# Row operands of TensorE as high and low part on two partitions, in one fp32r matmul

## What is computed

```python
# FoX: cum = cumsum(log_sigmoid(forget logits)), one row of 256 for each of 16 heads
s = einsum('bhqd,bhkd->bhqk', q_b, k) * scale
s = s + c_b[..., :, None] - cum[..., None, :]
# router: bias added to the logits of every token
p_group = softmax(xf @ wr_g + br_g);  e_logits = xf @ wr_e + br_e
# mixer: input projection with bias, q, k, v, o and others from column ranges of it
px = (rmsnorm(x, g) * (1 + sc1) + sh1) @ w_in + b_in
# mLSTM, chunk of 128: running maximum m_t of the log weights, decay to the state before
a = b + m;  Dlog = b[t] - b[s] + i[s];  m_t = max(a, max_s Dlog)
w_inter = exp(a - m_t);  s = (q k) * exp(Dlog - m_t)
num = w_inter * (q C) + s v;  den = w_inter * (q n) + sum(s)
```

## Time and profile before

| | us |
|---|---|
| median of three runs | 2669.48 |
| lowest, highest | 2665.62, 2684.37 |
| the profiled execution | 2661.06 |
| its span, first to last instruction | 2659.3 |

### The profile page before, as it was taken

One profiled execution on the slowest core, in us unless ns is written; L12 is line 12 of the kernel. 1 busy time (PEld: TensorE's weight loads), 2 busy tenths in 40 slices (PEclk: granted clock), 3 DMA queues, 4 the chain that ended last, 5 costly groups with the idle time before them and its releaser, 6 DMA issues. The chain is left out here.

```text
span 2659.3 us, 45347 instructions
## 1 busy us (share of the span) xinstructions
PE 2299.1 (86%) x19616; PEld 1828.5 (69%) x19616; DVE 1154.5 (43%) x2041; ACT 884.4 (33%) x1471; POOL 58.3 (2%) x78
## 2 busy tenths in 40 slices
PE   6999688888796799887999999886896998996998
PEld 6957465665462787675767676553766998866998
DVE  4344635323320552545323232333756554755554
ACT  4423232133210443332222221322534443534442
POOL 0000000000000000000000000000000000000000
PEclk9988898898998899988999999887888999988999
DMA  6575698899999556847999999976503644404650
GB/s 225 159 242 204 222 384 336 332 369 391 402 388 398 192 188 227 292 156 280 394 394 386 393 393 379 394 276 235 197 17 109 224 167 145 139 5 141 208 167 24
DMA packets 254368, 676.25 MB, mean 254 GB/s; under 512 B 12624, under 2 KB 65872, under 8 KB 254160
## 3 DMA queue, kind: packets, MB, share of 16 engines
q1 hardware_dynamic: 238832, 614.74, 62.5%
q0 software_dynamic: 15328, 58.50, 6.5%
HBM read 672.15 MB, written 1.05 MB: 253 GB/s over the span
## 5 line engine op out<-in xcount | busy, mean ns | idle before, releaser
L434 PE MATMUL bank<-xx,high 128*128 128x256 f32 (+1 forms) x3296 | 634.3, 294 | 59.5 <-DVE xx L570 37.1
L434 PEld LDWEIGHTS bank<-xx,high 128*128 128x128 f32 (+1 forms) x3296 | 524.6, 195 | 117.3 <-issue 76.7
L434 PE MATMUL bank<-xx,low 128*128 128x256 f32 (+1 forms) x1648 | 475.8, 289 | 0.0
L434 PEld LDWEIGHTS bank<-xx,low 128*128 128x128 f32 (+1 forms) x1648 | 321.8, 195 | 1.6
L385 DVE TENSOR_TENSOR low<-lane,high 128x1024 fp32r<-128x1024 f32 (+1 forms) x112 | 130.7, 1170 | 374.6 <-ACT high L376 374.6
L376 ACT ACTIVATE high<-lane 128x1024 fp32r<-128x1024 f32 (+1 forms) x112 | 112.9, 1012 | 334.0 <-PE bank L434 334.0
L434 PE MATMUL bank<-hx,high 128*128 128x256 f32 x1056 | 200.6, 291 | 6.3 <-DVE low L385 6.3
L434 PEld LDWEIGHTS bank<-hx,high 128*128 128x128 f32 x1056 | 166.5, 193 | 24.2 <-issue 15.2
L434 PE MATMUL bank<-hx,low 128*128 128x256 f32 x528 | 150.4, 285 | 0.0
L1229 ACT ACTIVATE hs<-bank 64x256 f32<-64x256 f32 x64 | 24.2, 377 | 312.3 <-PE bank L1216 312.2
L1236 DVE TENSOR_TENSOR hs<-hs,bank 64x256 f32<-64x256 f32 x64 | 27.1, 423 | 222.7 <-ACT hs L1229 222.5
(11 more groups left out here) (510 smaller groups left out, 4211.4 us busy)
## 6 DMA issues: line engine op xcount, KB each, us to landing
ring__11<-in_expert_w_gu SPq DMA_DIRECT2D x52, 1024.0 KB, 11.1
ring__10<-in_expert_w_gu SPq DMA_DIRECT2D x51, 1024.0 KB, 11.4
ring__12<-in_expert_w_gu SPq DMA_DIRECT2D x51, 1024.0 KB, 11.0
ring__50<-in_expert_w_gu SPq DMA_DIRECT2D x26, 1024.0 KB, 10.7
ring__10<-in_expert_w_down SPq DMA_DIRECT2D x26, 1024.0 KB, 9.1
ring__150<-in_expert_w_gu SPq DMA_DIRECT2D x26, 1024.0 KB, 12.0
ring__49<-in_expert_w_gu SPq DMA_DIRECT2D x25, 1024.0 KB, 10.8
ring__12<-in_expert_w_down SPq DMA_DIRECT2D x25, 1024.0 KB, 9.7
```

The source lines that it names most:

```text
L434: done = pe.matmul(out, a.bitcast(F32R), b.bitcast(F32R), start=it["start"] and k == 0 and q == 0 and not halves, stop=stop)
```

## The change

The row operands are put on two partitions (or two groups of them), as a high part rounded to fp32r and a low part, and one fp32r matmul adds both.

* **Inputs.** `row` arrives in a scratch tile, every bias on two partitions. ScalarE rounds all of it (128x1024), VectorE multiplies it by 0 or 1 on even or odd partitions (`odd`) and combines both (`flip` is +1 or -1): the even partition keeps the high part, the odd one gets the rest. FoX now waits for this last instruction (`stack`). ScalarE also makes fp32r copies of `ones` and of a new table `pick` (-1 where the partition modulo 32 is the head).
* **FoX.** `cum_s` holds the high part of cum and, 32 partitions on, the low part, for both halves; `pick` selects both and turns the sign. VectorE has a copy of 128x256 and two differences of 16x256 for one product of 128x256.
* **Mixer.** The directions sit at partitions 0 and 64 instead of 0 and 32. `nw` gets high parts at q0 and low parts at q0 + 32. A gate chain has four more instructions (18 counted steps for 14), with one more wait in each chunk. ScalarE clears `nw` (128x512) at the head of each mixer.
* `sgub` keeps an fp32 matmul, of two rows instead of one. `graw` becomes part of `tm`, and the context mixer shares the MoE's `rs`.

```diff
         def R(name, a=0, n=None):
             q, o, wd = ROW[name]
-            return row[q:q + 1, o + a:o + (wd if n is None else a + n)], ones[q:q + 1, :]
+            return row[q:q + 2, o + a:o + (wd if n is None else a + n)].bitcast(F32R), ones_r[q:q + 2, :].bitcast(F32R)
+        def picked(q, rows, h):
+            return pick[q:q + 32 + rows, h:h + 1].bitcast(F32R).to_broadcast([32 + rows, P])
...
             def act(act):
                 act.wait_ge(*vec_in.at("row"))
+                act.activation(ones_r.bitcast(F32R), ones, ACT.Copy)
+                act.activation(pick.bitcast(F32R), V("pick"), ACT.Copy)
                 act.activation(zeros.bitcast(F32R), V("mask_z"), ACT.Copy).then_inc(*zero_a.up("zeros"))
...
+                act.activation(rows_h.bitcast(F32R), rows, ACT.Copy).then_inc(*row_a.up("high"))
...
+                dve.tensor_scalar(rows_o, rows, V("odd"), None, MUL).then_inc(*row_v.up("odd"))
+                dve.wait_ge(*row_a.at("high"))
+                dve.wait_ge(*row_v.at("odd"))
+                dve.scalar_tensor_tensor(row.bitcast(F32R), rows_h, V("flip"), rows_o, MUL, ADD).then_inc(*row_v.up("stack"))
...
-            return room, [(x_out_a, ("in", 7)), (x_out, ("in", 6))], dict(sp=sp, pe=pe, act=act, dve=dve, pool=pool)
+            return room, [(x_out_a, ("in", 7)), (row_v, "stack")], dict(sp=sp, pe=pe, act=act, dve=dve, pool=pool)
...
-                    sel = ident[q0:q0 + H, q0 + h:q0 + h + 1]
-                    n = pe.matmul(sv[:, j, :], sel.to_broadcast([H, P]), ncum[q0:q0 + H, 0:nk], start=False, stop=True)
+                    n = pe.matmul(sv[:, j, :], picked(q0, H, h), cum_s[q0:q0 + 32 + H, 0:nk].bitcast(F32R), start=False, stop=True)
...
-                        dve.tensor_scalar(ncum, cum, -1.0, None, MUL).then_inc(*cum_v.up("ncum"))
+                        dve.tensor_copy(cum_s.bitcast(F32R), cum).then_inc(*cum_v.up("high"))
+                        dve.wait_ge(*cum_v.at("high"))
+                        for q0 in (0, 64):
+                            n = dve.tensor_tensor(cum_s[q0 + 32:q0 + 32 + H, :].bitcast(F32R), cum[q0:q0 + H, :], cum_s[q0:q0 + H, :], SUB)
+                        n.then_inc(*cum_v.up("ncum"))
...
-                pe.matmul(bank[:, 0:64], one, bc(rb[:, 4:36], [1, 2, 32], 1), start=True, stop=False, skip_group_check=True)
+                pe.matmul(bank[:, 0:64], one, bc(rb[:, 4:36], [2, 2, 32], 1), start=True, stop=False, skip_group_check=True)
...
             def decay_pe(pe, i, hp):
-                q0 = 32 * d
+                q0 = 64 * d
...
-                    sel = ident[q0:q0 + 4, q0 + h:q0 + h + 1].to_broadcast([4, P])
-                    n = pe.matmul(bank[:, 256 * j:256 * j + 256], sel, nw[q0:q0 + 4, a].rearrange("p c t -> p (c t)"), start=True, stop=True)
+                    n = pe.matmul(bank[:, 256 * j:256 * j + 256], picked(q0, 4, 2 * hp + j),
+                                  nw[q0:q0 + 36, a].rearrange("p c t -> p (c t)").bitcast(F32R), start=True, stop=True)
...
             def act(act):
                 events_wait(act, opened)
+                act.activation(nw.rearrange("p a c t -> p (a c) t").bitcast(F32R), bc(V("mask_z"), [P, 4, P], 1), ACT.Copy).then_inc(
+                    *gate_a.up(K("zero")))
                 norm.squares(act, 0)
...
-                    step(dve.tensor_scalar(NW[:, a, 0, :], MT[:, s0:s1], -1.0, None, MUL))
-                    yield
-                    step(dve.tensor_scalar(NW[:, a, 1, :], MT[:, s0:s1], -1.0, prev, MUL, ADD))
+                    step(dve.tensor_copy(NH[:, a, 0, :].bitcast(F32R), MT[:, s0:s1]))
+                    yield
+                    step(dve.tensor_scalar(NH[:, a, 1, :].bitcast(F32R), MT[:, s0:s1], prev, None, SUB))
+                    ready()
+                    step(dve.tensor_tensor(NL[:, a, 0, :].bitcast(F32R), MT[:, s0:s1], NH[:, a, 0, :], SUB))
+                    step(dve.scalar_tensor_tensor(NL[:, a, 1, :].bitcast(F32R), MT[:, s0:s1], prev, NH[:, a, 1, :], SUB, SUB))
```

More of the change, by code:

```diff
@@ L47 @@
                   ("mask_z", 128), ("mask_ge", 128), ("mask_le", 128), ("tri", 128), ("ones", 128), ("iota", 64), ("zero", 1),
-                  ("eps", 1), ("jota", NX)):
+                  ("eps", 1), ("jota", NX), ("flip", 1), ("odd", 1), ("pick", 16)):
     _vec(_name, _w)
@@ L160, in build @@
         vec = space(ctx, "vec", NVEC)
-        row = space(ctx, "row", NROW)
+        row, ones_r, pick = space(ctx, "row", NROW), space(ctx, "ones_r", P), space(ctx, "pick", 16)
         mods = space(ctx, "mods", 256)
@@ L192, in build @@
         zero_a = sig("zeros")
+        row_a, row_v = sig("rows_high"), sig("rows")
         tr_x, x_out = sig("x_turned"), sig("x_copied")
@@ L716, in inputs @@
             xin, cin = room("xin", 2, DM), room("cin", 2, DM)
+            rows, rows_h, rows_o = room("rows", NROW), room("rows_h", NROW), room("rows_o", NROW)
             groups = [(s, d, a, c) for s, d in ((xin, x), (cin, xr[:, :, 0:T])) for a in range(2) for c in (0, 4)]
@@ L720, in sp @@
                 sp.dma_start(vec, A["vec"]).then_inc(*vec_in.up("vec", 16))
-                sp.dma_start(row, A["row"]).then_inc(*vec_in.up("row", 16))
+                sp.dma_start(rows, A["row"]).then_inc(*vec_in.up("row", 16))
                 sp.dma_start(xin, A["x"][0].rearrange("(a p) d -> p a d", p=P)).then_inc(*x_in.up("x", 16))
@@ L776, in fox @@
             cum, ncum, wf = room("cum", T), room("ncum", T), room("wf", KC, P)
+            cum_s = room("cum_s", T)
             mod = Modulation(0, room)
@@ L1384, in pe @@
                 rb, one = R("br", 36 * L, 36)
-                pe.matmul(bank[:, 0:64], one, bc(rb[:, 4:36], [1, 2, 32], 1), start=True, stop=False, skip_group_check=True)
-                pe.matmul(bank[:, 64:72], one, bc(rb[:, 0:4], [1, 2, 4], 1), start=False, stop=False, skip_group_check=True)
+                pe.matmul(bank[:, 0:64], one, bc(rb[:, 4:36], [2, 2, 32], 1), start=True, stop=False, skip_group_check=True)
+                pe.matmul(bank[:, 64:72], one, bc(rb[:, 0:4], [2, 2, 4], 1), start=False, stop=False, skip_group_check=True)
                 pe.wait_ge(*rstd.at(norm.name))
@@ L1892, in norm_turns, with mixer @@
                     yield
-        def mixer(L, v, get, part, room, bk, opened, npairs, wide, rate, deep, early_in=None, x_ready=None, xx=None):
+        def mixer(L, v, get, part, room, bk, opened, npairs, wide, rate, deep, early_in=None, x_ready=None, xx=None, rs=None):
             K = lambda *k: (L, v, *k)
@@ L1977, in mixer @@
             end = len(proj.items) - 1
-            in_done = [(ev_a, proj.out(at_[where[-1]], last_o, 1)), (gate_v, K(0, 14)), (gate_v, K(1, 14)), (lastm_v, K(1))]
+            in_done = [(ev_a, proj.out(at_[where[-1]], last_o, 1)), (gate_v, K(0, 18)), (gate_v, K(1, 18)), (lastm_v, K(1))]
             if not states_only:
@@ L2038, in sgu_pe @@
                             pe.matmul(o, sv[:, a, g * 64:(g + 1) * 64], wst[:, g, :], start=True, stop=False, tile_position=(0, q0))
-                            n = pe.matmul(o, R("sgub")[1][:, 0:64], R("sgub", 512 * L + g * P, P)[0], start=False, stop=True,
+                            n = pe.matmul(o, ones[96:98, 0:64], R("sgub", 512 * L + g * P, P)[0].bitcast(F32), start=False, stop=True,
                                           tile_position=(96, q0))
@@ L2183, in gate_logs_act @@
                 for d in range(2):
[L2184 removed]
+                    B = rB[64 * d:64 * d + 4, :]
                     act.wait_ge(*gate_a.at(K(d, "exp")))
[L2186 removed]
+                    act.activation(B, B, ACT.Ln, bias=ones[64 * d:64 * d + 4, 0:1]).then_inc(*gate_a.up(K(d, "ln")))
             def conv_ln_act(act, which):
@@ L2334, in gate_chain @@
                 B, U, MT = (r_[q0:q0 + 4, :] for r_ in (rB, rU, rM))
-                NW, on4 = nw[q0:q0 + 4], ones[q0:q0 + 4, 0:1]
+                NH, NL, on4 = nw[q0:q0 + 4], nw[q0 + 32:q0 + 36], ones[q0:q0 + 4, 0:1]
                 dve.wait_ge(*gr_a.at(K(2 * d + 1)))
@@ L2772, in context_mixer @@
         def context_mixer(room, lane, bk, rs):
-            s = mixer(0, 0, room, room.part, lane, bk, [], 2, 256, 7, 1)[2]
+            s = mixer(0, 0, room, room.part, lane, bk, [], 2, 256, 7, 1, rs=rs)[2]
             def pool(e):
@@ L2950, in consts @@
         "tri": (p[:, None] < p[None, :]), "ones": np.ones((P, P)), "iota": np.tile(np.arange(64), (P, 1)),
+        "flip": np.where(p % 2 == 0, 1.0, -1.0)[:, None], "odd": (p % 2)[:, None], "pick": -1.0 * (p[:, None] % 32 == np.arange(16)),
         "zero": np.zeros((P, 1)), "eps": np.full((P, 1), EPS), "jota": np.tile(np.arange(NX), (P, 1)),
```

19 lines of the change are left out of this document (8 added, 11 removed).

## The result

Beside new runs of the kernel before (median 2667.55 us over 4), the changed kernel takes **2634.91 us** (2626.56 to 2638.48): a ratio of 0.986, 95% interval 0.983 to 0.989, faster by 1.4%. The forecast was 2646; the value lies inside its range, but outside "within 1%", which was called the likeliest (0.59; faster by over 1% had 0.35). The profiled executions took 2661.06 and 2636.17 us, their spans 2659.3 and 2634.3.

The account below looks back on a forecast made before the run. TensorE was taken to bound the FoX attention, expert-weight DMA the first MoE, and a chain of waits the x mixers. Nine parts sum to -23.2 us: 2637.9 on the profiled execution, 2646 on the median; range 2631 to 2661.

Parts of the forecast that it names:

- part 2: FoX attention, second query block: 16 matmuls of 256 columns each save 0.42 us, -6.7 us; bounds 4.9 and 8.
- part 3: FoX attention, first query block: 16 matmuls of 128 columns, half at each clock, -2.8 us; bounds 0 and 5.7.
- rival C: Slower by the clock: FoX's second query block falls to 1.2 GHz, up to +14 us or 2683; chance 0.05.
- part 1: Start: FoX waits for the stacked rows instead of the last copy of x, +2.0 us; bounds 1.5 to 3.
- part 6: x mixers, v and o biases: eight matmuls of 512 columns each save 0.74 us, -6.0 us; bounds 5 and 6.5.
- part 7: x mixers, decays: cheaper matmuls bring VectorE to num(0) 3.6 us earlier per mixer, -7.2 us; bounds -3 and -9.
- part 8: Mixers' gate chain: extra VectorE instructions and waits, partly absorbed by idle time, +2.0 us; bounds 0 and +5.
- part 9: ScalarE's clearing of `nw` at a mixer's head: hidden in the first x mixer, shows in the second, +0.5 us.
- parts 4, 5: First MoE, biases and decays beside a nearly full weight stream, -2 us; second MoE, in its starved stretch, -3 us.
- Rival D: fp32r matmuls of 2 to 48 rows cost the same four passes everywhere: +4.5 us, 2674; chance 0.05.
- A: More gets through: one pass at 128 columns, larger MoE gains, low fixed costs; about -36 us, 2633; chance 0.16.
- B: Gain stays small: FoX's first block and both MoEs give 0, fixed 0.2 stays; about -10 us, 2659; chance 0.14.

Follow-up runs that it names:

- the two traces with the other pattern: Kernel before with only the mixers' gates and decays changed (2675.99 us), and with only the stacked biases (2673.86 us); both keep the attention of before.
- the FoX runs: Kernel before with only FoX's forget-sum matmul edited: fp32r on 16 rows 2657.05 us, 32 rows 2652.14, 33 rows 2634.26; fp32 on 48 rows 2642.95.
- full-height bias: Kernel before plus the change's FoX part and biases, rows stacked early, decays as before, each bias matmul on 128 rows: 2624.62 us, later 2623.90.
- FoX alone: Kernel before with only the change's FoX hunks and the moved tiles that make room: 2630.92 us (ratio 0.987), later 2629.00.

## Why the prediction was right or wrong

**The step that failed is the FoX attention (parts 2 and 3).** It was put at -9.5 us and measured -27.7. The working took the 0.2 us over the passes for weight loads of the edited matmul alone, and had no term for a clock that rises. The runs showed in its place a change of mode of about 0.2 us, which the neighbours pay too (with 33 rows for 32 a head goes from 0.94 to 0.65 us), and with it the clock's return (0.63 to 0.95 in the first 36 us). All the rest was forecast at -13.7 together and came out at +2.7. That the sum of -23.2 was nearly met is luck.

**FoX, second block (part 2): right direction, the terms mis-sized.** Forecast 0.42 a matmul, 6.7 us. Measured (2.49 - 1.29)/2 = 0.60 a head, 9.6. The working took the 0.2 over four passes as weight loads, one of them gone, and only on the edited line. It was the change of mode, paid on the scores' side too; three passes less and more rows each bring about 0.3 a head.

**First block (part 3): the price was above its bound.** Two bounds were drawn, 0 and 0.26 a matmul at 2.4 GHz. A head went from 0.83 us (two matmuls of 0.41) to 0.37 (143.23 to 144.72 for four heads), so 0.46, 7.4 in all. The bound took the unedited neighbour as given.

**The clock (rival C): the wrong sign, and the largest term.** 27.7 less 9.6 and 7.4 leaves 10.7 us of the attention to the clock, and 20 or more against the 106.9 and 110.1 of the two traces with the other pattern. Rows 9 were read as "a full queue of short-row matmuls does not hold the upper level", which the FoX runs bear out, and then only a loss was made of it: less work, lower clock. The sign set for it, a clock of 175 to 222 us that leaves 0.98, looked at the second block, and what rose was the first. The first block's 0.75 in the earlier trace rows, with TensorE busy 47.5 of 48 us, was the sign that something in that block kept the clock down and that its removal could be worth up to a quarter of the block. It belonged among the gains. Why the clock follows the mode stays open.

**The base.** The sum was made against one execution, 8.4 us under the median, and then carried over to the median unchanged. If, as argued above, that execution did better than others in the attention, it did so in the very place that the change repairs.

**Start (part 1): right to 0.05 us as far as it was followed.** The stack was ready at 20.10 (forecast 20.15) and the squares came 2.3 later. What failed is the step from there: TensorE's longer idle cost it the clock for the sums, 1.7.

**x mixers, biases (part 6): the mechanism right, the price off.** 1.05 to 0.43, so 0.62 and not 0.74. The forecast took over half of the fixed 0.2 as gone beside three passes, and only the passes went, at 0.62/3 = 0.21 each. The Trainium skill, FP8 and Floating Point Precision, TensorE Precision Notes, gives true fp32 four passes, and the trace agrees. That fp32r takes one is read from the 0.233 of the earlier trace rows. The fixed part stays, as two rows beside 128 are still a change of mode.

**x mixers, decays (part 7): the path right, the price off.** Num(0) came after 8.7 us (forecast 9.5, before 13.3), since the work behind the decays waits for more, as forecast; but a decay took 0.16 and not 0.36, as the clock stood at 2.4 GHz there.

**Gate chain (part 8): too small.** +1.0 forecast, +2.8 and +2.6 measured. The 1.31 us of idle ahead of the low part of the earlier trace rows are still 1.31 after: that low part waits for ScalarE's high part, which had moved back with all the rest, so nothing was absorbed. Behind the later convolution sum TensorE's clock also comes back later: the 18 matmuls there take 5.87 us instead of 5.07.

**`nw` (part 9): right**, 0.5. **Feed-forward blocks: no term, and +5.5 beside `nw`.** The clock's fall ahead of the down projection, 3 us in each, was put at nothing, and its cause stays open. **MoEs (parts 4, 5):** -4.2 and about +2, inside what repeats of one kernel differ by; neither confirmed nor refuted.

**Rival D** (the same four passes) is refuted by 0.43 and 0.16 us; **A** and **B** were about sizes, and the sum came out beside them for another reason.

## What to carry to other kernels

Look at the number of rows of each small matmul and of its neighbours. Beside matmuls of 64 rows give it 33 to 64, beside 128 give it 128, with zero weights for the rest. The matmul got no longer by it (0.23 us for 128 rows of 512 columns), and each change of mode saved was 0.2 us. In FoX the clock rose as well; in the x mixer it fell earlier with the full-height bias, and the first one took 2 us more, so the whole has to be measured. Where a stretch has TensorE always busy and the clock well under 1.00, treat its return as a possible gain of any edit there, and compare the stretch in more than one execution before a forecast is hung on it.

## What the runs showed of the hardware

* The step between 32 and 33 rows beside a matmul of 64: 0.94 against 0.65 us a head at 256 columns, the clock of the first 36 us 0.63 against 0.95, the kernel 2652.1 against 2634.3.
* A change between matmuls of different row modes costs about 0.2 us: three less for two heads 0.56 to 0.58 us, two less at a bias 0.40.
* TensorE's clock mostly repeats with the program: in the FoX attention fp32r kernels with 16 and 32 rows have the same falls to 2 us, two traces of FoX alone too, while the third trace of the changed kernel has one fall more than the other two. A small edit shifts where it falls next. After an idle of 3.56 us ahead of FoX's sums the clock was down, which cost 1.7 us; after 3.17 us ahead of a down projection it fell in some kernels, at 3 us, and stayed up in others.
* 4x128 on VectorE beside GpSimd's 4x256: 0.60 us instead of 0.29.
